# A recurrence's score ladder: q and k kept decayed and multiplied by block totals, half-width matmuls and masked copies

## The reference, cut to what matters

```python
# q, k, logf: (B, S, H, dk); S_t = diag(f_t) S_{t-1} + k_t^T v_t ; o_t = q_t S_t
diff = G_[:, :, :, None, :] - G_[:, :, None, :, :]        # G: running sum of logf
decay = jnp.exp(jnp.where(incl[:, :, None], diff, -jnp.inf))
scores = jnp.einsum('bhtd,bhsd,bhtsd->bhts', q_, k_, decay)
out = jnp.einsum('bhts,bhse->bhte', scores, v_) + ...
```

## Time and profile before

| what | value |
|---|---|
| median of 3 runs | 1655.58 us (1654.44 to 1656.61) |
| profiled execution | 1656.24 us, span 1654.6 us |
| TensorE, VectorE, ScalarE, GpSimd busy | 84%, 65%, 47%, 6% of the span |
| mean granted TensorE clock | 0.908 |
| the ladder with its values' matmuls | 876.2 to 936.6 us of the span |

### The profile page before, as it was taken

How to read it: one execution, slowest core, us unless ns; L and a number is a source line. 1 busy time by engine, 2 the same in 40 slices (tenths; PEclk the granted TensorE clock), 3 DMA queues, 4 the chain that set the end, 5 groups by cost and what they waited for, 6 DMA issues and landing times.

```text
span 1654.6 us, 19024 instructions
## 1 busy us (share of the span) xinstructions
PE 1395.1 (84%) x7158; PEld 1183.7 (72%) x7158; DVE 1069.2 (65%) x1063; ACT 773.2 (47%) x757; POOL 100.0 (6%) x96
## 2 busy tenths in 40 slices
PE   4994899998996999978977567999969666799995
PEld 4973778886995788858966456888859545678884
DVE  7685477886765744443368646798864333678986
ACT  2673434333433343333453324677744542467772
POOL 0010000000000000000003113000012000300000
PEclk9997899998998999989986777999989877799998
DMA  9984269996743665543550032899937301189990
GB/s 362 355 287 161 77 218 311 308 308 213 259 161 103 204 191 190 177 153 115 166 178 1 1 91 73 284 347 351 349 121 256 103 0 51 51 287 321 347 356 36
DMA packets 205880, 327.64 MB, mean 198 GB/s; under 512 B 9504, under 2 KB 140256, under 8 KB 205808
## 3 DMA queue, kind: packets, MB, share of 16 engines
q1 hardware_dynamic: 192512, 276.71, 49.7%
q0 software_dynamic: 13296, 49.93, 8.9%
HBM read 325.56 MB, written 1.05 MB: 197 GB/s over the span
## 4 chain that ended last, share of the span: by engine, by line
PE 71%; DVE 16%; ACT 7%; issue 3%; DMA 1%; SPq 0%; DVEq 0%; ACTq 0%
PE ps L1829 21%; PE ps L1831 20%; PE ps L1830 20%; DVE w_low L1137 3%; ACT w_high L620 3%; PE ps L2357 1%; DVE scratch L1543 1%; DVE scratch L1525 1%; DVE scratch L1183 1%; PE ps L2271 1%; PE ps L1900 1%; PE ps L2028 1%; DVE h_low L1734 1%; PE ps L2074 1%; PE ps L2015 1%
## 5 line engine op out<-in xcount | busy, mean ns | idle before, releaser
L1137 DVE TENSOR_TENSOR w_low<-raw,w_high 128x2048 fp32r<-128x2048 f32 (+1 forms) x256 | 586.7, 2295 | 339.0 <-ACT w_high L620 337.0
L620 ACT ACTIVATE w_high<-raw 128x2048 fp32r<-128x2048 f32 (+1 forms) x256 | 484.4, 1895 | 414.1 <-PE ps L1831 386.8
L1829 PE MATMUL ps<-w_high,h_high 128*128 128x512 f32 (+1 forms) x928 | 368.6, 397 | 32.7 <-DVE h_low L1734 9.7
L1830 PE MATMUL ps<-w_low,h_high 128*128 128x512 f32 (+1 forms) x928 | 361.0, 389 | 0.0
L1831 PE MATMUL ps<-w_high,h_low 128*128 128x512 f32 (+1 forms) x928 | 360.7, 389 | 0.0
L1829 PEld LDWEIGHTS ps<-w_high,h_high 128*128 128x128 f32 x928 | 178.9, 193 | 70.8 <-DVE h_low L1734 10.5
L1831 PEld LDWEIGHTS ps<-w_high,h_low 128*128 128x128 f32 x928 | 178.3, 192 | 35.9
L1830 PEld LDWEIGHTS ps<-w_low,h_high 128*128 128x128 f32 x928 | 179.2, 193 | 33.4 <-issue 0.2
L1829 PE MATMUL ps<-h_high,w_high 128*128 128x256 f32 x624 | 183.0, 293 | 18.3 <-DVE h_low L1230 12.8
L1830 PE MATMUL ps<-h_low,w_high 128*128 128x256 f32 x624 | 181.0, 290 | 0.0
L1831 PE MATMUL ps<-h_high,w_low 128*128 128x256 f32 x624 | 180.8, 290 | 0.0
(11 more groups left out here) (307 smaller groups left out, 1438.2 us busy)
## 6 DMA issues: line engine op xcount, KB each, us to landing
raw<-in_w_down SPq DMA_DIRECT2D x124, 512.0 KB, 4.8
raw<-in_w_gate_up SPq DMA_DIRECT2D x88, 512.0 KB, 5.0
scratch<-in_w_ada POOLq DMA_DIRECT2D x40, 1024.0 KB, 5.5
raw<-in_w_gate SPq DMA_DIRECT2D x80, 512.0 KB, 4.4
raw<-in_w_up SPq DMA_DIRECT2D x80, 512.0 KB, 5.6
raw<-in_w_qkv SPq DMA_DIRECT2D x24, 512.0 KB, 12.8
raw<-in_w_o SPq DMA_DIRECT2D x24, 512.0 KB, 5.8
raw<-in_w_in SPq DMA_DIRECT2D x24, 512.0 KB, 4.9
```

The source lines that it names most:

```text
L620: act.activation(wh[u % SPL][:, :, 0:w], raw[u % RAW][:, :, 0:w], ACT.Copy).then_inc(h_split, 1)
L1137: dve.tensor_tensor(wl[u % SPL][:, :, 0:w], raw[u % RAW][:, :, 0:w], wh[u % SPL][:, :, 0:w].bitcast(F32), ALU.subtract).then_inc(l_split, 1)
L1829: pe.matmul(o, h1, h2, start=start, stop=False, skip_group_check=True)
L1830: pe.matmul(o, h1, l2, start=False, stop=False, skip_group_check=True)
```

## The change

`qd` and k are kept decayed. At level 1, `qd` is q times f, and k needs nothing. From one level to the next, the second half of each block of q is multiplied by the total decay of the block's first half, and the first half of each block of k by the total decay of the second half. These totals for all block sizes come from a tree of sums over log f made in chunk 5 on VectorE (six sums, 768 down to 24 elements per partition), with two exponentials on ScalarE, 1536 and 1512 elements. `kd`, `sfx` and GpSimd's product leave the ladder. k is used in place. TensorE's moving operand is the second half of each block alone, 64 stepped columns for 128, at levels 1 to 7, and the masked copy takes those 384 elements per partition for 768. Level 0 is computed from q and k themselves with the wide copy, and level 1's scores wait for nothing in the ladder.

```diff
+        def later(x, m):
+            return x.rearrange("p a (b x m) -> p a b x m", x=2, m=m)[:, :, :, 1, :]
+        def block_decay(m):
+            if m == 1:
+                return pfx
+            o = 18 * 256 + 1536 - 3072 // m
+            return W[:, o:o + 1536 // m].rearrange("p (h b) -> p h b", h=HG)
+        def pair_decay(m, hs, which):
+            return block_decay(m)[:, hs, :].rearrange("p h (b c) -> p (h b) c", c=2)[:, :, which:which + 1]
...
 GpSimd
-            for l in range(1, 9):
-                m = 2 ** (l - 1)
-                for u in range(2):
-                    hs = half_heads(u)
-                    pool.wait_ge(exp_ready, exr.up())
-                    pool.wait_ge(lev_scores, levs.up())
-                    pool.tensor_tensor(halves(kd[:, hs, :], m)[:, :, 0, :], level_exps(m, 1, u),
-                                       halves(kk[:, hs, :], m)[:, :, 0, :], ALU.mult).then_inc(kd_ready, 1)
...
 ScalarE, in the projection's loop
+                if c == 5:
+                    ahead(PLAN["a_in"] + 2 * c + 1)
+                    act.wait_ge(sums_ready, upd.up())
+                    act.activation(pfx, pfx, ACT.Exp).then_inc(act_step, 1)
+                    act.wait_ge(act_step, step.up())
+                    act.activation(W[:, 18 * 256:18 * 256 + 1512], W[:, 18 * 256:18 * 256 + 1512], ACT.Exp).then_inc(exp_ready, 1)
+                    act.wait_ge(exp_ready, exr.up())
...
 ScalarE, in the ladder
-                    if l > 1:
-                        act.wait_ge(sums_ready, upd.up())
-                        act.wait_ge(dk_ready, dqr.up())
-                        act.wait_ge(kd_ready, kdr.up())
-                    act.activation(level_exps(m, 0, u), halves(pfx[:, hs, :], m)[:, :, 1, :], ACT.Exp).then_inc(act_step, 1)
-                    act.wait_ge(act_step, step.up())
-                    act.activation(level_exps(m, 1, u), halves(sfx[:, hs, :], m)[:, :, 0, :], ACT.Exp).then_inc(exp_ready, 1)
...
 VectorE, in the projection's loop
-                    dve.tensor_copy(qd, q).then_inc(dve_step, 1)
...
                 if c == 5:
-                    dve.wait_ge(exp_ready, exr.up())
-                    dve.tensor_copy(kd, kk).then_inc(dk_ready, 1)
+                    for m in (1, 2, 4, 8, 16, 32):
+                        pairs = block_decay(m).rearrange("p h (b c) -> p h b c", c=2)
+                        dve.tensor_tensor(block_decay(2 * m), pairs[:, :, :, 0], pairs[:, :, :, 1],
+                                          ALU.add).then_inc(sums_ready if m == 32 else dve_step, 1)
+                        dve.wait_ge(sums_ready if m == 32 else dve_step, (upd if m == 32 else step).up())
+                if c == 6:
+                    dve.wait_ge(exp_ready, exr.up(2))
+                    dve.tensor_tensor(qd, q, pfx, ALU.mult).then_inc(dk_ready, 1)
                     dve.wait_ge(dk_ready, dqr.up())
-                    dve.memset(sfx, 0.0).then_inc(qk_in, 1)
...
 VectorE, in the ladder
+                elif l < 8:
+                    m = 2 ** (l - 1)
+                    dve.copy_predicated(
+                        later(scD[:, hs, :].rearrange("p h (c t) -> p (h c) t", c=2), m),
+                        later(mlev[:, l:l + 1, :], m).to_broadcast([P, HG, P // (2 * m), m]),
+                        ps[:, o, 0:3 * P].rearrange("p (a b m) -> p a b m", a=HG, m=m)).then_inc(lev_taken, 1)
...
-            for l in range(1, 9):
-                m = 2 ** (l - 1)
+            for l in range(9):
+                m = 2 ** max(l - 1, 0)
                 for u in range(2):
                     hs = half_heads(u)
-                    dve.wait_ge(exp_ready, exr.up())
                     dve.wait_ge(lev_scores, levs.up())
-                    dve.tensor_tensor(halves(qd[:, hs, :], m)[:, :, 1, :], level_exps(m, 0, u),
-                                      halves(q[:, hs, :], m)[:, :, 1, :], ALU.mult).then_inc(dk_ready, 1)
-                    dve.wait_ge(dk_ready, dqr.up())
-                    if l < 8:
-                        pv, sv, nb = halves(pfx[:, hs, :], m), halves(sfx[:, hs, :], m), 3 * S // (2 * m)
-                        dve.tensor_tensor(sv[:, :, 0, :], sv[:, :, 0, :],
-                                          pv[:, :, 1, m - 1:m].to_broadcast([P, nb, m]), ALU.add).then_inc(dve_step, 1)
+                    if 1 <= l < 8:
+                        qb, ka, nb = halves(qd[:, hs, :], m)[:, :, 1, :], halves(kk[:, hs, :], m)[:, :, 0, :], 3 * S // (2 * m)
+                        dve.tensor_tensor(qb, qb, pair_decay(m, hs, 0).to_broadcast([P, nb, m]), ALU.mult).then_inc(dve_step, 1)
                         dve.wait_ge(dve_step, step.up())
-                        dve.tensor_tensor(pv[:, :, 1, :], pv[:, :, 1, :],
-                                          pv[:, :, 0, m - 1:m].to_broadcast([P, nb, m]), ALU.add).then_inc(sums_ready, 1)
-                        dve.wait_ge(sums_ready, upd.up())
-                    take(l - 1, u)
-            for u in range(2):
-                dve.wait_ge(lev_scores, levs.up())
-                take(8, u)
+                        dve.tensor_tensor(ka, ka, pair_decay(m, hs, 1).to_broadcast([P, nb, m]), ALU.mult).then_inc(dk_ready, 1)
+                        dve.wait_ge(dk_ready, dqr.up())
+                    take(l, u)
...
 TensorE
-                    if l or not u:
+                    if l >= 2 or l == u == 0:
                         pe.wait_ge(dk_ready, dqr.up())
-                    if l:
-                        pe.wait_ge(kd_ready, kdr.up())
...
+                                if l:
+                                    m, c = 2 ** (l - 1), (2 * j + t) * (P // 2)
+                                    i = pe.matmul(ps[:, o, c:c + P // 2].rearrange("p (b m) -> p b m", m=m), kk[:, h, tok],
+                                                  later(qd[:, h:h + 1, tok], m)[:, 0, :, :], start=True, stop=True)
+                                else:
+                                    c = (j % 2) * S + t * P
+                                    i = pe.matmul(ps[:, o + j // 2, c:c + P], kk[:, h, tok], q[:, h, tok], start=True, stop=True)
```

More of the change, by code:

```diff
@@ L231, in build @@
         router_sums = sem("router_sums")
-        kd_ready = sem("kd_ready")
         sums_ready = sem("sums_ready")
@@ L340, in halves @@
             return x.rearrange("p h (b c m) -> p (h b) c m", c=2, m=m)
-        def level_exps(m, kind, u):
-            return Z[:, 768 * kind + 384 * u:768 * kind + 384 * u + 384].rearrange("p (b m) -> p b m", m=m)
+        def later(x, m):
[7 more added lines that the diff above has]
+            return block_decay(m)[:, hs, :].rearrange("p h (b c) -> p (h b) c", c=2)[:, :, which:which + 1]
         def half_heads(u):
@@ L889, in _ @@
             exr, dkr, upd = Count(exp_ready), Count(qk_in), Count(sums_ready)
-            dqr, kdr = Count(dk_ready), Count(kd_ready)
             for c in range(7):
+                if c == 5:
[5 more added lines that the diff above has]
+                    act.wait_ge(exp_ready, exr.up())
                 chunk_ready("a_in", c)
@@ L1497, in _ @@
                     dve.wait_ge(dve_step, step.up())
-                    dve.tensor_copy(qd, q).then_inc(dve_step, 1)
-                    dve.wait_ge(dve_step, step.up())
                 if c == 4:
@@ L1506, in _ @@
                 if c == 5:
-                    dve.wait_ge(exp_ready, exr.up())
-                    dve.tensor_copy(kd, kk).then_inc(dk_ready, 1)
+                    for m in (1, 2, 4, 8, 16, 32):
[6 more added lines that the diff above has]
+                    dve.tensor_tensor(qd, q, pfx, ALU.mult).then_inc(dk_ready, 1)
                     dve.wait_ge(dk_ready, dqr.up())
-                    dve.memset(sfx, 0.0).then_inc(qk_in, 1)
-                    dve.wait_ge(qk_in, dkr.up())
             ahead(PLAN["wo1"])
@@ L1523, in take @@
                 o, hs = level_bank(l, u), half_heads(u)
-                if l < 8:
+                if l == 0:
                     dve.copy_predicated(
@@ L1530, in take @@
                 dve.wait_ge(lev_taken, levt.up())
-            for l in range(1, 9):
-                m = 2 ** (l - 1)
+            for l in range(9):
+                m = 2 ** max(l - 1, 0)
                 for u in range(2):
                     hs = half_heads(u)
-                    dve.wait_ge(exp_ready, exr.up())
                     dve.wait_ge(lev_scores, levs.up())
-                    dve.tensor_tensor(halves(qd[:, hs, :], m)[:, :, 1, :], level_exps(m, 0, u),
-                                      halves(q[:, hs, :], m)[:, :, 1, :], ALU.mult).then_inc(dk_ready, 1)
-                    dve.wait_ge(dk_ready, dqr.up())
-                    if l < 8:
-                        pv, sv, nb = halves(pfx[:, hs, :], m), halves(sfx[:, hs, :], m), 3 * S // (2 * m)
-                        dve.tensor_tensor(sv[:, :, 0, :], sv[:, :, 0, :],
-                                          pv[:, :, 1, m - 1:m].to_broadcast([P, nb, m]), ALU.add).then_inc(dve_step, 1)
```

(26 more changed lines are left out.)

8 lines of the change are left out of this document (removed).

## The result

The changed kernel takes 1639.27 us (median of 5 runs, 1635.36 to 1642.51), against 1655.58 before (median of 5): a ratio of 0.9902, 95% interval 0.9882 to 0.9922, faster by 16.3 us. The forecast was 1642.1, with a range of 1631 to 1649.

A forecast was written before the change was run, and what follows sets the result against it. VectorE's ladder, held up by GpSimd, bound the kernel; afterwards TensorE's loads at half clock would. The values' matmuls ending at 923.05 against 936.60 gave 13.5 us off the 1655.6 median: 1642.1 us, range 1631 to 1649.

The forecast's parts named there:

- The ladder's bound: Recurrence's ladder: weight loads pace TensorE, so six matmuls take about 2.6 us at half clock, more than VectorE's 1.84.
- The time of the fall: TensorE's granted clock in the ladder: falls at about 887 us, as before, and stays down to the ladder's end.
- narrow matmuls do not hold the clock: TensorE in the ladder: narrow matmuls do not keep full clock, as in the router, busy 7.50 of 8 us at 0.54.
- unit 16's low half starts: VectorE ahead of the ladder: starts at 860.8, 1.2 us late on the chain, bounds 0.5 and 2.5.
- TensorE's level 0 starts: Ladder's first matmuls: start at 877.4 and not 876.2, because attention ends 1.2 us later.
- half-steps at half clock: Ladder levels 3 to 7: ten half-steps at 2.6 us, TensorE binding, ending at 912.6.
- values' matmuls: 36 records behind the ladder: 7.0 us, between 4.3 at full clock and 7.7 at half.
- VectorE's half-step: Ladder: two products of 0.56, a copy of 0.62 (bounds 0.56 and 1.02) and 0.10, together 1.84 us.
- Products stay at 1.24: Rival, VectorE in the ladder: form, not GpSimd, makes line 1543 slow; half-step 3.2 us, 1651 to 1655; chance 0.04.
- The clock stays full: Rival, ladder: VectorE binds throughout, 23.5 us earlier, 1632 (1638 if copies stay 1.02); chance 0.10.
- comes back midway: Rival, ladder: full clock for half the slow half-steps and the values, 6.5 us more gained, 1635.6; chance 0.18.
- Stepped read: Rival, TensorE in the ladder: stepped moving operand slows each record, 1668 at 0.43 us a record; chance 0.05.

The follow-up runs named there:

- Experiment 1: Changed kernel with TensorE's moving operand at levels 1 to 7 back at 128 contiguous columns, copy still 384 elements: 1631.99 us, ratio to before 0.9867.
- experiment 3: Changed kernel with the matmuls of the second half of the tokens left out at levels 1 to 7: 1631.52 us, ratio 0.9867.
- experiment 5: Changed kernel with 64-column matmuls at levels 1 to 3 and 128-column ones at levels 4 to 7: 1631.1 us in one run.
- experiment 6: Changed kernel with 128-column matmuls at levels 1 to 3 and 64-column ones at levels 4 to 7: 1635.4 us in one run.
- experiment 4: Changed kernel with second-half masks packed ahead, so the narrow masked copy reads its mask without steps: 1638.8 us in one run.
- experiment 8: The changed kernel as it is, run again beside two wide versions on one chip: 1636.76 us, ratio to before 0.9914.
- experiment 9: Changed kernel with 128 contiguous columns at levels 1 to 7, run again beside the changed kernel on one chip: 1632.36 us, ratio 0.9875.
- experiment 7: Kernel before with the product of line 569 moved from GpSimd to VectorE: 1651.1 us in one run, 1655.7 for the kernel before beside it.
- experiment 2: Changed kernel with an unused GpSimd product of 384 elements beside each half-step of levels 1 to 7: 1643.2 us in one run.

## Why the prediction was right

**The ladder's bound.** The step that mattered, that a record's pace does not go with its columns, that 12 x 0.213 us exceeds VectorE's 1.84, and that the clock falls near 887 and stays down, came out as written: 2.57 us for a forecast 2.6, ten such half-steps, fall at 887.4. Experiment 1 takes the fall of the clock away and experiment 3 half of the records, and in both VectorE binds again at 1.79 us. The Trainium skill ("TensorE: Matmul & The Clock Gate", section on LDWEIGHTS) gives a load as its columns divided by 1.2 GHz, 107 ns for 128, and makes no difference between the array's clocks. The runs do: 0.21 us a record at half clock.

The time of the fall was partly luck. The prediction took it from before, where it came 11.2 us after level 0's start (876.20 to 887.4); in the changed kernel it came 9.1 us after (878.29), and the later start made up for it. In the other profiles with narrow matmuls at the first levels it lies between 884.3 and 887.8. And one step had no reason behind it but the router's rows: that narrow matmuls do not hold the clock. Experiments 1, 5 and 6 bear it out.

**The terms, forecast and measured.**

| step | forecast | measured |
|---|---|---|
| unit 16's low half starts | 860.8 | 860.58 |
| TensorE's level 0 starts | 877.4 | 878.29 |
| VectorE's first product | 881.8 | 882.63 |
| half-steps at half clock | 10 x 2.6 | 10 x 2.57 |
| last copy ends | 916.05 | 917.80 |
| values' matmuls | 7.0 | 6.05 |
| they end | 923.05 | 923.92 |

The ladder and its surroundings gave 936.60 - 923.92 = 12.7 us where 13.5 were forecast. Two terms were off on the loss side. The attention got later by 1.14 us more than its delayed start, through the clock, as the 3.74 against 2.60 us show; the forecast had no term for it, though its bounds (0.5 to 2.5 for the delay) hold the 2.1 in all. And VectorE's half-step was not 1.84: products 2 x 0.56 as forecast, copy 0.58 for 0.62 at most levels, but 1.01 at the first four half-steps. For these 1.02 was the upper bound, though for a reason, the stepped mask, that experiment 4 refutes. It cost 0.4 us on each of the two half-steps that stand ahead of level 3 on the path, 0.8 in all; level 3 started at 888.31 and not 886.6 by that and by the late start of 0.83. (The 886.6 is two half-steps and the products of the third, 881.8 + 2 x 1.84 + 1.15; three half-steps, as the prediction has it, would be 887.3.) Behind that TensorE bound, and the copies' time was hidden. The values' matmuls gave 0.95 back: 7.0 was a guess between 4.3 and 7.7, and the clock came back at 921.6, 3.7 us after they began.

**The rest of the gain.** The forecast of 1642.1 lies 2.8 us above the median, although the stage that it reasons about gave 0.8 us less than it said: the rest of the program gave more. The forecast let everything behind the ladder move as one. It did not. The start of a SyncE load of the changed kernel, at three places behind the ladder.

```profile
952.77 0.38 SPq L399 DMA_DIRECT2D raw<-in_w_gate  x1
...
1366.30 0.38 SPq L399 DMA_DIRECT2D raw<-in_w_gate  x1
...
1442.53 0.38 SPq L399 DMA_DIRECT2D raw<-in_w_gate  x1
```

The same loads start at 966.60, 1383.56 and 1462.02 in before: 13.8, 17.3 and 19.5 us earlier. The step from 12.7 to 13.8 lies in the sums of squares, six records that took 5.49 us in before at a clock of 0.50 and 4.11 in the changed kernel at 0.68. Behind the first load the code is the same. Over the second layer's attention, 86 us of before (1298 to 1384), the mean granted clock was 0.72; over its 83 us in the changed kernel (1284 to 1367) it was 0.75, and 2.8 us were won there; over the 78 us from the second load to the third it was 0.76 in before and 0.78 over 76 us in the changed kernel, and 2.2 us were won. So of the 19.7 us of this profile 5.7 lie in work that the change doesn't touch, most of them where the clock was higher. That this is luck of the run and no part of the change is argued and not shown. Taking off what each run was ahead or behind at 746 us, the same loads are 16.1, 17.2 and 19.5 us earlier in experiment 8, and 23.3, 20.5 and 20.5 in experiment 9, so the tail moves both ways; in experiment 7, which has the ladder of before, it won 2.3; five runs of one kernel spread over 7 us. The 12.7 us itself repeats: in experiment 8 the values' matmuls end at 921.33, 12.7 us earlier once the 2.6 of its head start are taken off. The medians, 16.3 us apart here and 15.7 in experiment 8, hold some 3 us more than that, and how much of this the change brings about is open.

**The rivals.** "Products stay at 1.24" fell on the 0.56 of the changed kernel and on experiments 2 and 7. "The clock stays full" and "comes back midway" did not happen, and experiments 1 and 5 are what they would have been: ladders of 28.1 and 29.8 us. "Stepped read": 12 records of 64 stepped columns took 1.55 us at full clock against 1.60 of 128 contiguous ones, so the step costs nothing that shows at this pace.

## What to carry to other kernels

Before halving a matmul's moving side, look for rows with still fewer columns: if those go at the same pace, something else than the columns sets it, here most likely the weight load, and nothing is won. Narrower matmuls can then lose the clock and double the price of every record, so that the wide version, with half its output thrown away, is the faster, here by 4.4 us. Where two engines' operations of one size differ in time by a factor of two, see what a third engine does under the slow one before putting it down to its form, and put work that only has to be done early where its engine is idle, not in front of the next instruction on the path.

## What the hardware showed unexpectedly

The masked copy of 384 f32 from PSUM takes 1.01 us when it writes runs of 1 or 2 elements and 0.57 from runs of 4 on, whatever the steps of mask and source, while products with the same stepped operands and results in SBUF stay at 0.56. A GpSimd product of 384 elements and a VectorE product of the same size never ran together: whichever had begun first went through at its usual time, and the other ended late (experiment 2, in both orders). Copies from PSUM ran beside GpSimd at their usual 1.01 us.

Wide matmuls with gaps of up to 0.64 us between bursts of 1.60 us held the clock at 1.00 for 21 us (888.2 to 909.8 in experiment 1), where before, with bursts of the same twelve records every 3.51 us, it was at 0.50 for most of the time. With 64 columns for 128 and the same gaps it fell.
